# The opening of a one-layer backbone step: order of loads, norm products and the first two FFN chunks

## The chip, the cores and the metric

One core of one Trainium2 chip. The metric is the device time of one execution in microseconds (us). An execution is one launch that computes the whole step. TensorE (PE in the rows) does the matrix products, VectorE (DVE), ScalarE (ACT) and GpSimd (POOL) the rest; SyncE (SP) and ACT issue DMAs. MB is 1,048,576 bytes: each weight tile that is loaded is one.

## The reference, cut to what matters

One layer over 128 context tokens and 128 latent tokens, width 2048, fp32:

```
mod = silu(c) @ ada_w + ada_b            # 9 vectors of 2048 per token group
x += 0.5 * g1 * swiglu(rms_norm(x) * w * (1 + sc1) + sh1)      # FFN 1, hidden width 5632
z  = (rms_norm(x) * w * (1 + sc2) + sh2) @ w_in  -> mLSTM, attention, merge, w_out
x += g2 * mix
x += 0.5 * g3 * swiglu(rms_norm(x) * w * (1 + sc3) + sh3)      # FFN 2
swiglu(h) = (silu(g) * u) @ wo   with g, u = split(h @ wi, 2)
```

The change touches only the start: the modulation vectors sc1 and sh1, the first norm, and the first two column chunks (512 wide) of g and u of FFN 1.

## The kernel before, in words

**Units and tiles.** A weight tile `raw_w` is 512 rows by 512 columns, 1 MB, four slots. Each tile makes two units. Every product is done in three single passes: the weight is split into `w_hi` (ACT, line 1278) and `w_lo` (DVE, line 1731), the activation into `xT_hi` and `xT_lo`, and a unit (line 672) is 2 row blocks by 2 token groups by 3 matmuls: 12 matmuls of 512 columns, over 256 rows of the contraction. `w_hi` and `w_lo` have four slots, so a unit's split waits for the product four units earlier. SP may issue the load of a raw tile when both units of the tile four before it are split (`tile`, line 389).

**The modulation chunks.** A chunk of `ada_w` (2048 by 512) is four tiles of 1 MB, called quarters of the chunk here, ada 0 to ada 8. `ada_q(c, q)` (line 592) is the product of one of them with the conditioning vectors, 4 matmuls with 32 weight columns (8 records in the trace). After the fourth, DVE adds the bias (`ada_rows`), PE selects two rows (`ada_sel`), DVE copies (`ada_blk`), PE transposes (`ada_T`), DVE copies to columns (`ada_cols`). `ada_w_sb` has one slot per quarter, so the load of a quarter waits until PE has used the same quarter of the chunk before (`ada_used`, lines 383 and 386); two more slots, `ada_x`, take the first two quarters of ada 3, 5 and 7.

**The first FFN in four quarters.** Quarter q of the model width (512 of 2048) needs ada 2q and 2q+1: they give the scale and the shift of this quarter's part of x. So `norm0_quarter(q)` (DVE line 1817, ACT line 1330) makes `acol`, modulates `xm`, and splits it into `xT_hi` and `xT_lo`; only then can PE run the units of the quarter. On DVE the order is: acol, xm, the split of the quarter's first unit, `xT_lo`. PE's `prologue` (line 761) runs, for each q, six units (G0, U0 and G1: gate chunk 0, value chunk 0, gate chunk 1, two units each), between them the products of the two ada chunks of the next quarter, and then, in `second` (line 796), the eight units of U1, value chunk 1, over all four quarters. The accumulators are PSUM banks 0 and 1 (G0, later free), 2 and 3 (U0, later U1), 4 and 5 (G1); bank 6 takes the ada products, bank 7 the selections.

**The start.** ACT issues the small loads (identity, `colrows`, `biasrows`) and then the tokens x; SP issues ada 0 at once. PE transposes `colrows` and `biasrows` when all of the small loads have landed, ACT makes the conditioning vectors (silu), PE runs ada 0, then ACT's sums of squares and DVE's `variance` and `diagonal` give `diag`, and PE makes the normed, transposed tokens as products with `diag` (`norm0`, line 661, eight banks), with ada 1 among them (lines 888 to 905).

**What sets the order.** It is all written out by hand: each engine works its own list in order, and waits at semaphores. SP's list of loads is lines 413 to 427: ada 0, ada 1, three tiles, ada 2, ada 3, three tiles, and so on, then ada 8 in halves between the four tiles of U1. A load that must wait holds up all loads behind it on SP.

Of the kernel before, what the change touches and what calls it, by code (L numbers as in the profile page):

```python
# [75 lines left out]
QT = 6  # L76
VCH = 4 * SC3
# [66 lines left out]
def build(nc, I, O):  # L144
    ctx = ExitStack()
    with ctx:
# [54 lines left out]
        vec_acc = place("vec_acc", [P, GROUPS, CH], at=SLOT + 32768)  # L201
        assert top[0] <= SCR
# [96 lines left out]
        ctile_zeroed = sem("ctile_zeroed")  # L299
        bias_zeroed, xm_act, acol_ready = sem("bias_zeroed"), sem("xm_act"), sem("acol_ready")  # L300
# [66 lines left out]
        def _(sp):  # L367
# [30 lines left out]
            def ffn(f, t0):  # L398
# [14 lines left out]
                if f == 0:  # L413

                    for q in range(4):
                        ada_load(2 * q)
                        if q == 0:
                            sp.wait_ge(bias_zeroed, 1)
                            bias(0)
                        ada_load(2 * q + 1)  # L420
                        for n, col in enumerate((0, D_FF, CH)):
                            tile(t0 + 3 * q + n, 0, rows(wi, q)[:, :, col:col + CH])
                    for q in range(4):
                        if q < 2:
                            ada_load(ADA_PRE, (2 * q, 2 * q + 1))
                        tile(t0 + 12 + q, 0, rows(wi, q)[:, :, CH + D_FF:2 * CH + D_FF])
                    ffn_out(0, t0 + 16, 0)
                else:
                    ffn_in(0, t0, 0)
# [161 lines left out]
        def _(pe):  # L591
# [114 lines left out]
            def ffn(f, u0, stage):  # L706
# [55 lines left out]
                def prologue():  # L762

                    for q in range(4):
                        a, b = 2 * q + 2, 2 * q + 3
                        for m in range(QT):
                            if q < 3 and m == 4:
                                if q == 0:
                                    pe.wait_ge(xn_act, 4)
                                ada_sel(a, a)  # L770
                                ada_q(b, 0)
                                ada_T(a)
                                for r in range(1, 4):
                                    ada_q(b, r)
                            kb = 4 * q + 2 * (m % 2)
                            pe.wait_ge(xT_lo_ready, kb // 2 + 1)
                            for half in range(2):
                                if q < 3 and m == 4 and half == 1:
                                    ada_sel(b, b)
                                unit(u0 + QT * q + m, 0, xT_hi, xT_lo, kb, 2 * (m // 2), kb == 0, kb == KD - 2, (half,))  # L780
                                if q == 0 and m == 2 and half == 0:
                                    ada_q(a, 2)
                                if q == 0 and m == 2 and half == 1:
                                    ada_q(a, 3)
                                if 0 < q < 3 and m == 3 and half == 0:
                                    ada_q(a, m)
                            if q < 3 and m == 4:
                                ada_T(b)
                            if q == 0 and m == 0:
                                pe.wait_ge(xn_dve, 4)  # L790
                            if q < 3 and m < (3 if q else 2):
                                ada_q(a, m)
                            if q == 3 and m >= 4:
                                ada_q(ADA_PRE, m - 4)

                def second():

                    def u_between(k):
                        if k < 2:
                            ada_q(ADA_PRE, k + 2)  # L800
                        if k == 1:
                            pe.wait_ge(silu_done, 2)
                            h_transposes(0)

                    pe.wait_ge(h_done, 1)
                    x_chunk(u0 + 24, 0, 2, u_between)
                    ffn_out(0, u0 + 32, 0)
                    ada_sel(ADA_PRE, ADA_PRE)
                    h_transposes(1)

                if f == 0:
                    prologue()
                    second()
# [75 lines left out]
            pe.wait_ge(rows_landed, 96)  # L889
            pe.transpose(ps[:, 0, 0:80], colrows[:, :], cst[0:80, C_ID:C_ID + 80])  # L890
            pe.transpose(ps[:, 0, 80:188], biasrows[:, :], cst[0:108, C_ID:C_ID + 108]).then_inc(cols_ps, 1)
            pe.wait_ge(cond_silu, 1)
            pe.wait_ge(one_ready, 1)
            ada_acc(0)
            ada_sel(0, 0)
            ada_T(0)
            norm0(range(4))
            ada_acc(1)
            ada_sel(1, 1)
            norm0(range(4, 6))  # L900
# [365 lines left out]
        def _(act):  # L1266
# [63 lines left out]
            def norm0_quarter(q):  # L1330
# [4 lines left out]
                split(QT * q, 0)  # L1335
# [12 lines left out]
                split(QT * q + 1, 0)  # L1348
# [41 lines left out]
            def ffn(f, u0):  # L1390
# [47 lines left out]
                def prologue():  # L1438

                    for q in range(4):  # L1440
                        norm0_quarter(q)
                        if q == 0:
                            xn_copy(3)
                        for m in range(2, QT):
                            split(u0 + QT * q + m, 0)
                    act.wait_ge(units_done, u0 + 20)
# [1002 lines left out]
```

## Time and profile before

| | |
|---|---|
| time, median of 3 runs | 2241.32 us (2240.49 to 2242.13) |
| span of the profiled execution, first to last instruction | 2238.6 us |
| median time less that span | 2.7 us |
| PE busy | 2209.0 us, 99% |
| DVE busy | 1606.5 us, 72% |
| ACT busy | 935.3 us, 42% |
| read from memory | 543.71 MB (decimal), 244 GB/s over the span |
| granted TensorE clock, mean | 0.999 |

The profiled execution's own time is not given apart from its span; the 2.7 us around the span are the launch and the end, as far as the median tells. A busy share counts an engine as busy until the modelled end of its instruction; for a matmul of 512 columns that is 0.39 us, while the next one starts 0.23 us after it. So the start times are what to read on PE, and an idle time in the rows is a little shorter than the gap between the starts.

### The profile page before, as it was taken

How to read it: one execution, taken by the hardware profiler on the slowest of the kernel's cores; microseconds unless marked ns; L12 is line 12 of the kernel's file. 1: busy time of each engine (PE TensorE's matmuls, PEld its weight loads, DVE VectorE, ACT ScalarE, POOL GpSimd, SP SyncE). 2: the span in 40 equal slices, each digit the busy share in tenths (PEclk: the TensorE clock that was granted, in tenths of full speed). 3: DMA queues.
4: the chain of work that ended last, by engine and by line, in shares of the span. 5: the costliest groups of instructions: out<-in, count | busy, mean ns of one | idle time of the engine just before them, and what ended most of it. 6: DMA issues, size and time to landing. Idle time of an engine off the chain costs nothing.

```text
span 2238.6 us, 28359 instructions
## 1 busy us (share of the span) xinstructions
PE 2209.0 (99%) x10498; PEld 1773.5 (79%) x10498; DVE 1606.5 (72%) x1858; ACT 935.3 (42%) x1099; POOL 64.5 (3%) x55
## 2 busy tenths in 40 slices
PE   6999999999999999999999999999999999999999
PEld 3567877878778778888888888888888888888887
DVE  3447888878887879756867887885567676776756
ACT  3334333333333336445544444454434443444443
POOL 0010000000000000000600000100000000000000
PEclk9999999999999999999999999999999999999999
DMA  9998888778888786655536776746675757557563
GB/s 371 387 326 312 283 315 299 278 278 302 308 280 291 276 267 211 215 163 167 185 113 227 260 264 228 269 162 207 221 241 193 261 191 258 192 188 262 188 225 131
DMA packets 273332, 548.13 MB, mean 245 GB/s; under 512 B 9014, under 2 KB 9418, under 8 KB 273008
## 3 DMA queue, kind: packets, MB, share of 16 engines
q1 hardware_dynamic: 212388, 421.59, 55.2%
q10 hardware_dynamic: 57772, 115.57, 14.4%
q0 software_dynamic: 3104, 10.05, 1.6%
q8 instruction: 45, 0.74, 0.1%
q14 instruction: 23, 0.19, 0.0%
HBM read 543.71 MB, written 3.46 MB: 244 GB/s over the span
## 4 chain that ended last, share of the span: by engine, by line
PE 96%; DMA 2%; DVE 2%; ACT 1%; issue 0%; SPq 0%; ACTq 0%; DVEq 0%
PE ps L681 30%; PE ps L683 29%; PE ps L682 29%; DMA ada_w_sb<-in_ada_w 2%; PE ps L618 1%; PE ps L603 1%; PE ps L758 1%; PE ps L627 1%; PE ps L668 0%; PE ps L1032 0%; PE ps L1100 0%; DVE w_lo L1731 0%; PE ps L635 0%; PE ps L1108 0%; DVE xm L1846 0%
## 5 line engine op out<-in xcount | busy, mean ns | idle before, releaser
L1278 ACT CAST w_hi<-raw_w 128x1024 fp32r<-128x1024 f32 x728 | 764.7, 1053 | 1169.4 <-PE ps L683 1110.9
L1731 DVE TENSOR_TENSOR w_lo<-raw_w,w_hi 128x1024 fp32r<-128x1024 f32 x728 | 897.3, 1236 | 442.9 <-ACT w_hi L1278 438.9
L681 PE MATMUL ps<-w_hi,xT_hi 128*128 128x512 f32 x2080 | 821.4, 395 | 4.2 <-DVE xT_lo L1814 3.4
L683 PE MATMUL ps<-w_hi,xT_lo 128*128 128x512 f32 x2080 | 810.5, 390 | 0.0
L682 PE MATMUL ps<-w_lo,xT_hi 128*128 128x512 f32 x2080 | 810.0, 389 | 0.0
L681 PEld LDWEIGHTS ps<-w_hi,xT_hi 128*128 128x128 f32 x2080 | 390.8, 188 | 110.3 <-issue 25.0
L683 PEld LDWEIGHTS ps<-w_hi,xT_lo 128*128 128x128 f32 x2080 | 390.5, 188 | 82.9
L682 PEld LDWEIGHTS ps<-w_lo,xT_hi 128*128 128x128 f32 x2080 | 390.9, 188 | 78.4
L1786 DVE SCALAR_TENSOR_TENSOR vec_acc<-ada_w_sb,ctile,vec_acc 128x512 f32<-128x512 f32 x420 | 299.1, 745 | 0.0
L681 PE MATMUL ps<-w_hi,hT_hi 128*128 128x512 f32 x704 | 276.2, 392 | 0.0
L683 PE MATMUL ps<-w_hi,hT_lo 128*128 128x512 f32 x704 | 274.2, 390 | 0.0
L682 PE MATMUL ps<-w_lo,hT_hi 128*128 128x512 f32 x704 | 273.9, 389 | 0.0
L683 PEld LDWEIGHTS ps<-w_hi,hT_lo 128*128 128x128 f32 x704 | 132.1, 188 | 27.8
L681 PEld LDWEIGHTS ps<-w_hi,hT_hi 128*128 128x128 f32 x704 | 132.2, 188 | 26.9 <-issue 0.2
L682 PEld LDWEIGHTS ps<-w_lo,hT_hi 128*128 128x128 f32 x704 | 132.2, 188 | 26.8
L1936 DVE TENSOR_TENSOR acc<-acc,ps 128x1024 f32<-128x1024 f32 x72 | 87.9, 1221 | 48.3 <-PE ps L683 48.3
L681 PE MATMUL ps<-w_hi,hcT_hi 128*128 128x512 f32 x128 | 50.1, 391 | 0.0
L683 PE MATMUL ps<-w_hi,hcT_lo 128*128 128x512 f32 x128 | 49.9, 390 | 0.0
L682 PE MATMUL ps<-w_lo,hcT_hi 128*128 128x512 f32 x128 | 49.8, 389 | 0.0
L1786 DVE SCALAR_TENSOR_TENSOR vec_m<-ada_m,ctile,vec_m 128x512 f32<-128x512 f32 x60 | 43.2, 746 | 0.0
L512 POOL DMA_DIRECT2D gate_dram<-gate_rows x3 | 1.6, 538 | 1414.8 <-DVE gate_rows L1742 1414.8
L603 PE MATMUL ps<-ada_w_sb,ctile 128*32 128x512 f32 x240 | 35.4, 678 | 7.1 <-DMA ada_w_sb<-in_ada_w 6.8
(279 smaller groups left out, 1036.8 us busy)
## 6 DMA issues: line engine op xcount, KB each, us to landing
raw_w<-in_ffn_wi SPq DMA_DIRECT2D x176, 1024.0 KB, 5.1
ada_w_sb<-in_ada_w ACTq DMA_DIRECT2D x96, 1024.0 KB, 8.2
raw_w<-in_ffn_wo SPq DMA_DIRECT2D x88, 1024.0 KB, 5.2
raw_w<-in_w_in SPq DMA_DIRECT2D x68, 1024.0 KB, 5.3
ada_w_sb<-in_ada_w SPq DMA_DIRECT2D x30, 1024.0 KB, 12.5
raw_w<-in_w_out SPq DMA_DIRECT2D x16, 1024.0 KB, 5.3
ada_m<-in_ada_w ACTq DMA_DIRECT2D x12, 1024.0 KB, 5.3
raw_w<-in_w_proj_m SPq DMA_DIRECT2D x8, 1024.0 KB, 5.3
```

What stands on the lines that cost most here:

```text
L512: pool.dma_start(gate_dram[r].rearrange("k g p -> (k g) p"), gate_rows[:, at, :]).then_inc(gate_stored, 16)
L603: mm = pe.matmul(ps[32 * j:32 * j + 32, 6, :], ctile[:, 4 * q + j, :], w[:, q, j, :], start=(q == 0), stop=(q == 3))
L618: mm = pe.matmul(ps[32 * j:32 * j + 32, 6, :], ctile[:, 4 * q + j, :], ada_w_sb[:, t, j, :], start=(q == 0), stop=(q == 3))
L627: mm = pe.transpose(ps[:, bank + g, b * P:(b + 1) * P], vec[:, g, b * P:(b + 1) * P], ident)
L681: pe.matmul(out, a_hi, w_hi[:, slot, kk, :], start=(first and kk == 0), stop=False)
L682: pe.matmul(out, a_hi, w_lo[:, slot, kk, :], start=False, stop=False)
L683: mm = pe.matmul(out, a_lo, w_hi[:, slot, kk, :], start=False, stop=(last and kk == 1))
L758: mm = pe.transpose(ps[:, 4 + b // 2, (b % 2) * TOK + g * P:(b % 2) * TOK + (g + 1) * P], h[:, g, b * P:(b + 1) * P], ident)
L1278: act.copy(w_hi[:, us % SPL, :, :], raw_w[:, slot, 2 * half:2 * half + 2, :]).then_inc(hi_ready, 1)
L1731: dve.tensor_tensor(w_lo[:, us % SPL, :, :], raw_w[:, slot, 2 * half:2 * half + 2, :], w_hi[:, us % SPL, :, :].bitcast(F32), ALU.subtract) ...
L1786: ins = dve.scalar_tensor_tensor(acc[:, g, :], w, scale, acc[:, g, :], ALU.mult, ALU.add)
L1936: dve.tensor_tensor(acc[:, :, c], acc[:, :, c], ps[:, banks:banks + 2, :], ALU.add).then_inc(acc_done, 1)
```

## The change

In words:

- The tokens are issued by SP ahead of ada 0 (they were issued by ACT behind the small loads). The bias rows have a semaphore and a PSUM bank of their own, so that the conditioning vectors wait only for `colrows`.
- The norm products of banks 0 to 3 run between the second and third quarter of ada 0, bank 4 and 5 around the selection of ada 0, then ada 1, then bank 6 and 7. DVE makes `diag` ahead of `ada_rows(0)`.
- The tiles of the first two FFN chunks come in a new order (`PRE_TILES`). Quarter 0 runs G0, U0 and U1; then U1, G0, U0 of quarter 1; then G1 of quarters 0 and 1; then G0, U0, G1 of quarter 2 and of quarter 3; then U1 of quarters 2 and 3. The quarters' first units are 0, 6, 16 and 22 (they were 0, 6, 12 and 18).
- U1 of quarters 0 and 1 is summed in banks 4 and 5, ACT copies it to `u1_half`, and G1 takes the banks. U1 of quarters 2 and 3 is summed in banks 2 and 3, and DVE adds the two halves in an instruction of its own ahead of `h`.
- SP's list becomes: x, ada 0, ada 1, tiles 0 to 2, ada 2, ada 3, tiles 3 to 6, ada 4, tile 7, ada 5, tiles 8 to 10, ada 6, ada 7, tiles 11 to 15, ada 8.
- On PE ada 4 and ada 5 stand among units 10 to 14, ada 6 and 7 among 16 to 21. The transposes of ada 3 and ada 7 stand behind units 5 and 21.

```diff
+PRE_TILES = ((0, G_0), (0, U_0), (0, U_1), (1, U_1), (1, G_0), (1, U_0), (0, G_1), (1, G_1),
+             (2, G_0), (2, U_0), (2, G_1), (3, G_0), (3, U_0), (3, G_1), (2, U_1), (3, U_1))
+Q_UNIT = (0, 6, 16, 22)
+PRE_BANKS = {G_0: 0, U_0: 2, G_1: 4, U_1: 4}
...
+                    sp.dma_start(x[:, CTX, :], I["x_prompt"][0]).then_inc(x_landed, 16)
+                    sp.dma_start(x[:, LAT, :], I["x_sample"][0]).then_inc(x_landed, 16)
+                    ada_load(0)
+                    sp.wait_ge(bias_zeroed, 1)
+                    bias(0)
+                    ada_load(1)
+                    pre_tiles(0, 3)
+                    ada_load(2)
+                    ada_load(3)
+                    pre_tiles(3, 7)
+                    ada_load(4)
+                    pre_tiles(7, 8)
+                    ada_load(5)
+                    pre_tiles(8, 11)
+                    ada_load(6)
+                    ada_load(7)
+                    pre_tiles(11, 16)
+                    ada_load(ADA_PRE)
...
+                    whole(0)
+                    pe.wait_ge(xn_dve, 4)
+                    whole(1)
+                    ada_q(2, 0)
+                    whole(2)
+                    ada_q(2, 1)
+                    whole(3)
+                    ada_q(2, 2)
+                    ada_q(2, 3)
+                    pe.wait_ge(xn_act, 4)
+                    pre_unit(4, 0)
+                    ada_sel(2, 2)
+                    ada_q(3, 0)
+                    ada_T(2)
+                    pre_unit(4, 1)
+                    ada_q(3, 1)
+                    ada_q(3, 2)
+                    ada_q(3, 3)
+                    whole(5)
+                    ada_sel(3, 3)
+                    ada_T(3)
+                    whole(6, 7, 8, 9)
+                    ada_q(4, 0)
+                    whole(10)
+                    ada_q(4, 1)
+                    whole(11)
+                    pe.wait_ge(u1_half_copied, 1)
+                    whole(12)
+                    ada_q(4, 2)
+                    ada_q(4, 3)
+                    pre_unit(13, 0)
+                    ada_sel(4, 4)
+                    pre_unit(13, 1)
+                    ada_q(5, 0)
+                    ada_T(4)
+                    for r in range(1, 4):
+                        ada_q(5, r)
+                    under_two(5, 14)
+                    for m in range(16, 20):
+                        whole(m)
+                        ada_q(6, m - 16)
+                    pre_unit(20, 0)
+                    ada_sel(6, 6)
+                    ada_q(7, 0)
+                    ada_T(6)
+                    for r in range(1, 4):
+                        ada_q(7, r)
+                    pre_unit(20, 1)
+                    ada_sel(7, 7)
+                    whole(21)
+                    ada_T(7)
+                    whole(22, 23, 24, 25, 26, 27)
+                    pe.wait_ge(h_done, 1)
+                    whole(28, 29)
+                    pe.wait_ge(silu_done, 2)
+                    h_transposes(0)
+                    ada_q(ADA_PRE, 0)
+                    ada_q(ADA_PRE, 1)
+                    whole(30)
+                    ada_q(ADA_PRE, 2)
+                    ada_q(ADA_PRE, 3)
+                    whole(31)
                     ffn_out(0, u0 + 32, 0)
...
+            ada_q(0, 0)
+            ada_q(0, 1)
+            norm0(range(4))
+            ada_q(0, 2)
+            ada_q(0, 3)
+            norm0(range(4, 5))
+            pe.wait_ge(biascol_copied, 3)
             ada_sel(0, 0)
+            norm0(range(5, 6))
             ada_T(0)
             ada_acc(1)
             ada_sel(1, 1)
             ada_T(1)
             norm0(range(6, 7))
...
+                        if q == 1:
+                            act.wait_ge(units_done, u0 + 8)
+                            act.copy(u1_half[:], ps[:, 4:6, :]).then_inc(u1_half_copied, 1)
...
+                    dve.tensor_tensor(u1_half[:], u1_half[:], ps[:, 2:4, :], ALU.add).then_inc(u1_summed, 1)
...
+                    dve.tensor_tensor(h[:], sg[:], u1_half[:], ALU.mult).then_inc(h_done, 1)
```

`whole(m)` is one unit, `pre_unit(m, half)` half of one, and `under_two(c, m)` is half of unit m, `ada_sel(c)`, the other half, `ada_T(c)` and unit m + 1.

## Rows read from the trace of the kernel before

**Rows 1.** The page: busy time, and the 40 equal slices of 56 us.
```profile
PE 2209.0 (99%) x10498; PEld 1773.5 (79%) x10498; DVE 1606.5 (72%) x1858; ACT 935.3 (42%) x1099; POOL 64.5 (3%) x55
...
PE   6999999999999999999999999999999999999999
...
DMA  9998888778888786655536776746675757557563
```

**Rows 2.** Stages by time: length, engines' busy time, granted clock, DMA share, GB/s.
```profile
0.00:25.00 25.00, 9.19 (x43) 1.67 (x43) 4.34 (x20) 8.39 (x22) 0.20 (x4) 1.00 0.96 355
...
75.00:100.00 25.00, 22.88 (x130) 11.81 (x128) 6.97 (x15) 2.89 (x4) 0.00 (x0) 0.93 1.05 387
...
125.00:150.00 25.00, 24.05 (x111) 17.34 (x110) 14.65 (x19) 14.95 (x18) 0.89 (x1) 1.00 1.05 387
150.00:175.00 25.00, 25.00 (x121) 18.97 (x120) 11.97 (x11) 9.08 (x9) 6.56 (x11) 1.00 0.87 256
```

**Rows 3.** PE's timeline, opening: start us, us, instruction, idle before it and releaser.
```profile
19.72 1.94 PE L603 MATMUL ps<-ada_w_sb,ctile 128*32 128x512 f32 x8 [0.78 <-DMA ada_w_sb<-in_ada_w]
...
25.73 5.79 PE L668 MATMUL ps<-diag,x 128*128 128x128 f32 x32 [1.66 <-DVE diag L1805]
31.45 3.64 PE L603 MATMUL ps<-ada_w_sb,ctile 128*32 128x512 f32 x32
...
41.79 0.50 PE L681 MATMUL ps<-w_hi,xT_hi 128*128 128x512 f32 x1 [1.59 <-DVE xT_lo L1814]
...
61.59 1.06 PE L603 MATMUL ps<-ada_w_sb,ctile 128*32 128x512 f32 x8 [0.36 <-DMA ada_w_sb<-in_ada_w]
...
69.64 0.50 PE L681 MATMUL ps<-w_hi,xT_hi 128*128 128x512 f32 x1 [0.59 <-DVE xT_lo L1814]
...
88.67 1.06 PE L603 MATMUL ps<-ada_w_sb,ctile 128*32 128x512 f32 x8 [0.47 <-DMA ada_w_sb<-in_ada_w]
91.39 1.93 PE L603 MATMUL ps<-ada_w_sb,ctile 128*32 128x512 f32 x8 [1.66 <-DMA ada_w_sb<-in_ada_w]
...
100.96 0.50 PE L681 MATMUL ps<-w_hi,xT_hi 128*128 128x512 f32 x1 [0.58 <-DVE xT_lo L1814]
...
121.21 1.06 PE L603 MATMUL ps<-ada_w_sb,ctile 128*32 128x512 f32 x8 [0.84 <-DMA ada_w_sb<-in_ada_w]
...
129.29 0.50 PE L681 MATMUL ps<-w_hi,xT_hi 128*128 128x512 f32 x1 [0.58 <-DVE xT_lo L1814]
...
132.70 0.47 PE L681 MATMUL ps<-w_hi,xT_hi 128*128 128x512 f32 x1 [0.36 <-DVE w_lo L1731]
...
173.88 0.39 PE L681 MATMUL ps<-w_hi,hT_hi 128*128 128x512 f32 x1
```

**Rows 4.** PE's timeline: two ada products around one unit, a transpose of ada.
```profile
72.58 1.07 PE L603 MATMUL ps<-ada_w_sb,ctile 128*32 128x512 f32 x8
...
76.53 1.06 PE L603 MATMUL ps<-ada_w_sb,ctile 128*32 128x512 f32 x8
...
97.34 0.27 PE L642 MATMUL ps<-cst,ada_rows_sb 128*128 128x128 f32 x1
```

**Rows 5.** SP's timeline: start us, us over all, DMA issues.
```profile
12.70 9.39 SPq L387 DMA_DIRECT2D ada_w_sb<-in_ada_w  x4
...
81.61 2.95 SPq L387 DMA_DIRECT2D ada_w_sb<-in_ada_w  x2
```

**Rows 6.** The page's DMA issues: count, KB each, median us to landing.
```profile
raw_w<-in_ffn_wi SPq DMA_DIRECT2D x176, 1024.0 KB, 5.1
```

**Rows 7.** ACT's timeline: the first and the last of eight sums of squares.
```profile
16.22 0.63 ACT L1319 ACTIVATE sg<-x 128x512 f32<-128x512 f32 x1 [4.06 <-DMA x<-in_x_sample]
...
20.52 0.61 ACT L1319 ACTIVATE sg<-x 128x512 f32<-128x512 f32 x1
```

**Rows 8.** DVE's timeline: the second product of silu and value.
```profile
174.20 1.21 DVE L2032 TENSOR_TENSOR h<-sg,ps 128x1024 f32<-128x1024 f32 x1
```

**Rows 9.** A short stretch with its granted clock, columns as in rows 2.
```profile
92.00:94.00 2.00, 2.00 (x10) 0.66 (x3) 0.61 (x1) 0.00 (x0) 0.00 (x0) 0.50 1.05 388
```

More of the change, by code:

```diff
@@ L201, in build @@
         vec_acc = place("vec_acc", [P, GROUPS, CH], at=SLOT + 32768)
+        u1_half = place("u1_half", [P, GROUPS, CH], at=SLOT + 32768)
         assert top[0] <= SCR
@@ L413, in ffn, with pre_tiles @@
                 if f == 0:
[L415 to L426, printed above, removed]
+                    def pre_tiles(first, end):
+                        for n in range(first, end):
+                            q, col = PRE_TILES[n]
+                            tile(t0 + n, 0, rows(wi, q)[:, :, col:col + CH])
+                    sp.dma_start(x[:, CTX, :], I["x_prompt"][0]).then_inc(x_landed, 16)
[16 more added lines that the diff above has]
+                    ada_load(ADA_PRE)
                     ffn_out(0, t0 + 16, 0)
@@ L762, in prologue @@
                 def prologue():
[L764 to L803, printed above, removed]
-                    pe.wait_ge(h_done, 1)
-                    x_chunk(u0 + 24, 0, 2, u_between)
+                    def pre_unit(m, half):
+                        q, col = PRE_TILES[m // 2]
+                        kb = 4 * q + 2 * (m % 2)
+                        pe.wait_ge(xT_lo_ready, kb // 2 + 1)
+                        first, last = kb == 0 or (col, kb) == (U_1, KD // 2), kb == KD - 2 or (col, kb) == (U_1, KD // 2 - 2)
+                        banks = 2 if col == U_1 and q > 1 else PRE_BANKS[col]
+                        return unit(u0 + m, 0, xT_hi, xT_lo, kb, banks, first, last, (half,))
@@ new lines, in whole, with under_two @@
+                    def whole(*ms):
+                        for m in ms:
+                            pre_unit(m, 0)
+                            mm = pre_unit(m, 1)
+                        return mm
+                    def under_two(c, m):
+                        pre_unit(m, 0)
+                        ada_sel(c, c)
+                        pre_unit(m, 1)
+                        ada_T(c)
+                        whole(m + 1)
+                    whole(0)
+                    pe.wait_ge(xn_dve, 4)
@@ L812, in ffn @@
                     prologue()
-                    second()
                 else:
@@ L1443, in prologue @@
                             xn_copy(3)
-                        for m in range(2, QT):
-                            split(u0 + QT * q + m, 0)
-                    act.wait_ge(units_done, u0 + 20)
+                        for m in range(Q_UNIT[q] + 2, Q_UNIT[q] + QT):
+                            split(u0 + m, 0)
+                        if q == 1:
+                            act.wait_ge(units_done, u0 + 8)
+                            act.copy(u1_half[:], ps[:, 4:6, :]).then_inc(u1_half_copied, 1)
+                            for m in range(12, 16):
+                                split(u0 + m, 0)
+                    act.wait_ge(units_done, u0 + 24)
                     act.activation(sg[:], ps[:, 0:2, :], ACT.Silu).then_inc(silu_done, 1)
-                    for u in range(24, 24 + AHEAD):
-                        split(u0 + u, 0)
-                    act.wait_ge(units_done, u0 + 24)
+                    for m in range(28, 28 + AHEAD):
+                        split(u0 + m, 0)
+                    act.wait_ge(units_done, u0 + 28)
                     act.wait_ge(h_done, 1)
                     act.activation(sg[:], ps[:, 4:6, :], ACT.Silu).then_inc(silu_done, 1)
-                    for k in range(16):
-                        split(u0 + 24 + AHEAD + k, 0)
-                        if k == 2:
+                    for m in range(28 + AHEAD, 40 + AHEAD):
+                        split(u0 + m, 0)
+                        if m == 33:
                             hT_hi_of(0)
-                        if k == 4:
+                        if m == 35:
                             act.wait_ge(ada_used, 4 * VCH1)
@@ L2008, in prologue @@
                         norm0_quarter(q)
-                        for m in range(2, QT):
-                            split(u0 + QT * q + m, 0)
+                        for m in range(Q_UNIT[q] + 2, Q_UNIT[q] + QT if q != 1 else Q_UNIT[2]):
+                            split(u0 + m, 0)
                         if q < 3:
@@ L2083, in _ @@
                 xn_copy(n)
+            ada_rows(0, 0, 16)
+            xn_copy(2)
+            ada_blk(0)
+            ada_cols(0)
             ada_rows(1, 1, 16)
             ada_blk(1)
-            xn_copy(2)
             ada_cols(1)
```

57 lines of the change are left out of this document (28 added, 29 removed).

## The prediction

> **What bounds the kernel now.** I read the page first: PE is busy 99% of the span, and of its 40 slices only the first is under 9 tenths [rows 1]. So all that an edit of the opening can give is PE's lost time in the first 150 us. The stages by time come next: up to 150 us the DMA share is 1.05 at 387 GB/s, its full rate, and PE has holes; from 150 us PE is busy 25.00 of 25 us [rows 2]. So there are two bounds, one behind the other: first the stream of loads, then PE without a gap to the end. A microsecond that PE gets ahead by the end of the opening is one off the total, and a microsecond lost there stays lost.
>
> PE's timeline shows the holes [rows 3]. Until the first unit at 41.79 it waits for loads, for diag and for xT_lo. From the first unit of quarter 1 (69.64) to the first unit of the output product (173.88) it takes 104.24 us, in which the holes are 0.47, 1.66 and 0.84 (a quarter of ada not landed), 0.58 twice (xT_lo of quarters 2 and 3) and 0.36 (w_lo): 4.49. To this comes time at half clock: the ada product at 91.39 takes 1.93, not 1.06, and the stage 92 to 94 has a granted clock of 0.50, 1.2 of 2.4 GHz [rows 3, 9]. With some 0.65 on the first matmuls of the next unit that is 1.5. So 6.0 us are lost, and 98.2 are work.
>
> **The stream of loads sets the quarters.** The last quarter of ada 3 is the 21st MB, that of ada 5 the 32nd, that of ada 7 the 43rd (2 of x, 4 per chunk of ada, 3 tiles per quarter). PE was released by them at 61.59, 91.39 and 121.21 [rows 3]: 29.8 us per 11 MB, 2.71 per MB. Quarter 1 starts 8.05 after the first of these.
>
> **The change part by part.**
>
> *Start.* The tokens go ahead of ada 0, so the sums of squares, 16.22 to 21.1 before [rows 7], can start at about 10 to 12, and diag is there at some 16.6 to 18.7 (25.7 before). PE's norm products then fill holes between the quarters of ada 0. ada 1 still ends as the 10th MB, at 19.72 + 4 x 2.71 = 30.6 at the earliest. The four ada 1 products, 31.45 to 35.1 before, now end at about 31.6, the transpose follows at once, and the first unit comes some 4 us earlier, at 37 to 38. Yet this buys nothing: quarter 1 hangs on ada 3, and ada 3 is still the 21st MB. PE already waited for it by 0.36; it will wait about 2. I take nothing for the whole start, though it moves 9 us of idle time.
>
> *A cost in it.* SP may load quarter 3 of ada 1 only when PE has used quarter 3 of ada 0. In the kernel before SP issued its four loads from 12.70 on and the share never fell [rows 5, 2]. Now 32 norm products (5.79 us, half of them slow [rows 3]) stand ahead of that use, which comes at diag (16.6 to 18.7) + 5.8 + 1.0 = 23.4 to 25.5. A load into an empty stream takes 5.1 us to land [rows 6]: 28.5 to 30.6, against 27.9 in an unbroken stream. So the stream stops for 0.6 to 2.7 us, and everything behind it on SP with it. It could be 0 if x lands very early. I take 1.5.
>
> *Quarter 0.* Now unit 5 runs ahead of the selection and transpose of ada 3, so nothing covers the chain behind the transpose. From the landing of ada 3: product 1.0, unit 5 with its start 2.84, selection to copy 0.6, copy to transpose to columns 0.7, and from columns to the first unit 3.3. That is 8.4 against 8.05: +0.4, and a hole of about 3.3 in place of 0.59. Bounds 0 to 0.9.
>
> *Quarter 1.* Ten units and ada 4 and 5. From unit 6 at about 70 (plus the 1.5): a unit with an ada product takes 3.95 (76.53 less 72.58 [rows 4]), without 2.73. So ada_q(4,2) comes after 7 units and 2 products, at some 93.3 (it was 81.5). SP must wait for it with quarter 3 of ada 5, whose issue was at 81.61 [rows 5]; with the quarters 1 and 2 of ada 5 landed by 91.2, the stream runs dry for some 3 us, and ada 5 ends at 101.2, not 96.6. PE arrives there at 100.5: a wait of 0.7. From then all loads are late, and the last of ada 7, now the 45th MB, comes at 101.2 + 11 x 2.71 = 131.0, where PE is at 129.9: 1.1. Together 1.8 us; 0 if the stream doesn't stop, up to 3.4 if issue costs more. This takes the place of 0.47 + 1.66 + 0.84 and the 1.5 at half clock.
>
> *Quarter 2 to 3.* Between transpose of ada 5 and unit 16 stands one unit, as before: 0.58. But ada 7's transpose stands behind unit 21 with nothing after it. From a transpose to the next quarter's first unit 3.62 pass (97.34 to 100.96 [rows 3, 4]), so PE stands for 3.35 where it stood 0.58. That is the largest new hole.
>
> *Small terms.* Units 6 to 9 and 22 to 27 follow without an ada product between the first two, so the w_lo wait of 0.36 [rows 3] comes twice. ada 8 and part of ada 4 run in pairs (1.0 each rather than 1.2): -0.7, bounds 0 and -1.2.
>
> *u1_half.* ACT's copy of two banks (about 1.05) is done long before unit 12 asks for it. DVE's addition (1.2, as h [rows 8]) comes behind unit 31, then h; PE's second part of the output product asks for h two units, 5.5 us, later, and 2.6 are needed. Nothing; were the cover gone, 1.2. Nor does ada 8 at the end of SP's list matter: with all stops it has landed by 160, and PE uses it from 162 on.
>
> *Sum against the span of 2238.6.* Start 0; stop of the stream +1.5; quarter 0 +0.4; from quarter 1 on the holes are 0.58 + 3.35 + 0.72 + 1.8 - 0.7 = 5.75 in place of 6.0: -0.25. Together +1.65. The profiled span lies 2.7 under the median of the timed runs, and I carry the difference over: 2241.3 + 1.65 = 2243.0. The low end of the terms (no stop, no late ada) is 0.4 + 4.65 - 0.7 - 6.0 = -1.65; the high end, 0.4 + 2.7 + 0.58 + 3.35 + 0.72 + 3.4 - 0.7 - 6.0, is +4.45.
>
> **The rivals.**
>
> *The reordering works as a whole.* Behind the last quarter's release now 11.5 units are left, not 15.5: 10.9 us less work behind a landing that is 2 MB, 5.4 us, later. Read so, the gain would be 5.5. It speaks for this that the DMA waits are the longest holes. Against it: only 6.0 us are lost at all from quarter 1 on, and 3.35 of new waiting is written into the order. With the stream unbroken I get -1.65, 2239.7; with the new hole shrunk to 0.58 as well -4.4, 2236.9. Chance 0.17.
>
> *SP stands behind PE (slower).* The place is SP's wait for ada_q(0,2) and ada_q(4,2), the price is each stop in full (up to 2.7 and 3.4), and it decides once the stops add up to over 3 us: +4.45, 2245.8. For it: SP's list is strictly in order. Against: the share held at 1.05 through all of its waits so far. Chance 0.16.
>
> *Half clock.* In the opening PE fell to 1.2 GHz once, at about 91.5, after waits of 0.47 and 1.66 with one ada product between them, and was back at full clock by 96 [rows 3, 9]; the xT_lo wait of 1.59 at 41.79 brought no fall. The new holes of 3.3 are longer than any after 41.79. If one brings a fall like that one, +1.5; if both do, +3: 2244.5 or 2246.0. Chance 0.17.
>
> The Trainium skill ("TensorE: Matmul & The Clock Gate", What's actually happening) says that half rate is the default state and that activity alone lifts it, so idle stretches send the clock back. The trace agrees in the one case that it has. By that rule the longer holes should each cost this; by the row of 41.79 a hole alone doesn't.
>
> **How the numbers follow.** The forecast (stops of 1 to 3 us, both holes, no fall) has 0.50, its own range 2241 to 2244.5. About 0.2%, 4.5 us, is what a measurement can tell from no change. Faster than 2236.8 needs the first rival and more: 0.07. Slower than 2245.8 takes the second rival's upper half, both falls, or a mix: 0.17. The rest, 0.76, is within. The range is 2238.0 to 2247.5: it takes in the low sum and most of a stop with a fall.
>
> **What would show it.** First unit at 37 to 39 (41.79 before) but the first unit of quarter 1 at 69.5 to 72. A dip of the DMA share near 25 us and near 91 to 96. PE idle about 3.3 ahead of unit 6 and of unit 22, released by xT_lo, the latter at 140 to 142. First output unit at 174 to 177 (173.88 before). No change of PE after it. I am wrong if quarter 1 starts clearly before 69, if the share stays at 1.05 to 130, or if something after 175 us moves.

## The result, and the profile after

| | before | changed |
|---|---|---|
| median of 8 runs | 2241.01 us | 2247.09 us |
| lowest to highest | 2240.29 to 2242.13 | 2245.12 to 2248.30 |
| span of the profiled execution | 2238.6 us | 2243.2 us |

The changed kernel is slower: ratio 1.0026, 95% interval 1.0017 to 1.0035, +6.1 us. The forecast was 2243.0. The profiled execution of the changed kernel is the quickest of its eight (2245.12); its span is 4.6 above that of before, and the trace accounts for these 4.6. The other runs of it have spans up to 2246.4. Time less span is 1.7 to 2.1 us in the runs on record, not the 2.7 that the text ahead of the prediction gives; there a span and a median of different executions were compared.

PE's timeline of the changed kernel, the lines that answer to [rows 3] (start us, us, instruction, idle before it and releaser; the changed kernel has line 623 for 603, 688 for 668, 701 for 681):

```profile
18.22 5.29 PE L688 MATMUL ps<-diag,x 128*128 128x128 f32 x32 [1.62 <-DVE diag L1877]
...
33.73 1.07 PE L623 MATMUL ps<-ada_w_sb,ctile 128*32 128x512 f32 x8 [2.88 <-DMA ada_w_sb<-in_ada_w]
...
63.57 1.07 PE L623 MATMUL ps<-ada_w_sb,ctile 128*32 128x512 f32 x8 [0.60 <-DMA ada_w_sb<-in_ada_w]
...
72.04 0.50 PE L701 MATMUL ps<-w_hi,xT_hi 128*128 128x512 f32 x1 [3.35 <-DVE xT_lo L1886]
...
105.57 1.07 PE L623 MATMUL ps<-ada_w_sb,ctile 128*32 128x512 f32 x8 [1.64 <-DMA ada_w_sb<-in_ada_w]
113.65 0.50 PE L701 MATMUL ps<-w_hi,xT_hi 128*128 128x512 f32 x1 [0.58 <-DVE xT_lo L1886]
135.22 1.06 PE L623 MATMUL ps<-ada_w_sb,ctile 128*32 128x512 f32 x8 [0.81 <-DMA ada_w_sb<-in_ada_w]
...
144.64 0.79 PE L701 MATMUL ps<-w_hi,xT_hi 128*128 128x512 f32 x1 [3.35 <-DVE xT_lo L1886]
...
178.44 0.39 PE L701 MATMUL ps<-w_hi,hT_hi 128*128 128x512 f32 x1
```

The last line is the one to start from: the output product begins at 178.44, not 173.88, 4.56 later, and the whole span is 4.6 longer. So nothing behind it moved, and everything is in the opening. Quarter 1 starts at 72.04 (69.64 before): +2.4. From there to the output product it is 106.40 (104.24 before): +2.16.

Short stages of the changed kernel (columns as in [rows 2]: length, busy of PE, PEld, DVE, ACT, POOL, granted clock, DMA share, GB/s):

```profile
24.00:26.00 2.00, 2.00 (x22) 0.86 (x15) 0.57 (x1) 0.13 (x1) 0.00 (x0) 1.00 0.55 126
26.00:28.00 2.00, 2.00 (x26) 1.51 (x28) 1.01 (x3) 0.07 (x1) 0.00 (x0) 1.00 0.89 312
...
36.00:38.00 2.00, 1.58 (x14) 1.32 (x7) 1.03 (x5) 1.05 (x1) 0.00 (x0) 0.50 1.06 389
...
56.00:58.00 2.00, 2.00 (x14) 1.05 (x6) 0.69 (x1) 0.00 (x0) 0.00 (x0) 1.00 0.52 122
...
72.00:74.00 2.00, 1.96 (x6) 1.51 (x6) 0.69 (x1) 1.97 (x5) 0.00 (x0) 0.62 1.06 387
74.00:76.00 2.00, 2.00 (x6) 1.61 (x5) 1.91 (x2) 1.95 (x3) 0.00 (x0) 0.52 1.04 385
...
94.00:96.00 2.00, 2.00 (x15) 1.13 (x17) 1.05 (x1) 0.00 (x0) 0.00 (x0) 1.00 0.00 0
```

Two things are new. The first is the stream of loads. In the kernel before its share was 0.92 or more in every stage of 2 us from 20 to 154 us. Now the loads stop three times while PE still depends on them: at 24 to 28, at 56 to 58, and at 92 to 98 (the share is 0.00 in the stage shown). A fourth stop at 144 to 150 comes when no later row of the opening has a wait for a load. The second is the clock. Right behind the hole of 3.35 ahead of unit 6 most of the time is at 1.2 GHz (granted 0.62 and 0.52 in the two stages shown); the same follows behind the hole ahead of unit 22 (granted 0.54 in 144 to 146). There is a third such stretch ahead of both, from 34 to 41 us (0.50 in 36 to 38), behind the wait of 2.88 for ada 1. SP's timeline says what it stood behind in the second and the third stop:

```profile
55.87 1.23 SPq L396 DMA_DIRECT2D ada_w_sb<-in_ada_w  x2
...
77.89 4.60 SPq L393 DMA_DIRECT2D ada_x<-in_ada_w  x2
96.48 1.23 SPq L396 DMA_DIRECT2D ada_w_sb<-in_ada_w  x2
```

The pair at 55.87 is quarters 3 and 4 of ada 3, which wait for the products of ada 2 behind unit 3. From 82.5 to 96.5 SP issues nothing. The pair at 96.48 is quarters 3 and 4 of ada 5; in the kernel before they went out from 81.61 on [rows 5]. They wait for the products of ada 4 behind unit 12.

### The profile page after: what moved, and what is told of

Read it like the earlier page. It is cut to its first block, busy times and chain, and to the rows that moved or that the text cites. A ratio compares the mean times of both kernels' runs of the same rounds, so it can differ in the third digit from the quotient of the medians.

```text
span 2243.2 us, 28403 instructions
## 1 busy us (share of the span) xinstructions
PE 2209.6 (99%) x10498; PEld 1777.6 (79%) x10498; DVE 1608.3 (72%) x1859; ACT 936.4 (42%) x1100; POOL 64.5 (3%) x55
## 4 chain that ended last, share of the span: by engine, by line
PE 96%; DMA 2%; DVE 1%; ACT 1%; issue 0%; ACTq 0%; DVEq 0%
PE ps L701 30%; PE ps L703 29%; PE ps L702 29%; PE ps L638 1%; DMA ada_w_sb<-in_ada_w 1%; PE ps L623 1%; PE ps L778 1%; PE ps L647 1%; PE ps L688 0%; ACT sg L1388 0%; PE ps L1101 0%; PE ps L1169 0%; DMA colrows<-in_norm_ffn_w 0%; PE ps L655 0%; PE ps L1177 0%; DVE xm L1918 0%
```

## The experiments

The figures are medians of 11 runs (9 of e12), against the median of the kernel before on the same chip; the intervals of the ratios are about 0.0009 to each side, 2 us. So a difference between two experiments of under 2 us rests on their runs and traces more than on its interval.

| kernel | median us | against before | ratio, 95% interval |
|---|---|---|---|
| changed kernel | 2247.09 | +6.1 | 1.0026 (1.0017 to 1.0035) |
| e1 norm products behind ada 0 | 2245.24 | +4.2 | 1.0017 (1.0008 to 1.0026) |
| e2 both transposes early | 2244.01 | +2.9 | 1.0012 (1.0003 to 1.0021) |
| e3 ada 4 used early | 2245.42 | +4.4 | 1.0019 (1.0010 to 1.0028) |
| e4 holes filled | 2244.56 | +3.5 | 1.0017 (1.0008 to 1.0026) |
| e5 start alone | 2243.61 | +2.4 | 1.0010 (1.0001 to 1.0019) |
| e6 last transpose early | 2244.66 | +3.5 | 1.0015 (1.0006 to 1.0024) |
| e7 four edits | 2239.17 | -2.0 | 0.9992 (0.9983 to 1.0001) |
| e8 four edits and fill | 2237.51 | -3.7 | 0.9984 (0.9975 to 0.9993) |
| e9 as e8, old start | 2240.51 | -0.8 | 0.9998 (0.9989 to 1.0007) |
| e10 as e8, ada 3 in unit 5 | 2236.51 | -4.8 | 0.9980 (0.9971 to 0.9989) |
| e11 mended start alone | 2240.88 | -0.4 | 0.9999 (0.9990 to 1.0009) |
| e12 as e10, ada 7 in unit 20 | 2235.51 | -5.8 | 0.9975 (0.9965 to 0.9985) |

**e1: the first stop.**

```diff
-            ada_q(0, 0)
-            ada_q(0, 1)
-            norm0(range(4))
-            ada_q(0, 2)
-            ada_q(0, 3)
-            norm0(range(4, 5))
+            ada_acc(0)
+            norm0(range(5))
```

> The changed kernel with one edit: all four products of ada 0 ahead of the norm products (banks 0 to 4 then run behind them). Theory (stream stop): SP waits for quarter 3 of ada 0 to be used, so the stop of the load stream at 24 to 28 us goes, ada 3 lands at about 61.6 instead of 63.6, the first unit of quarter 1 starts at about 70.0 instead of 72.0, and the time falls by 2 us, to about 2245. Rival (the start is covered by the later stops and costs nothing): the landing of ada 3 moves, but unit 22 stays at 144.6 and the time within 0.5 us of 2247.

Measured: 2245.24, 1.9 less than the changed kernel. The share stays at 1.04 to 1.07 from 22 to 42 us. PE's timeline of e1:

```profile
38.96 0.50 PE L701 MATMUL ps<-w_hi,xT_hi 128*128 128x512 f32 x1 [1.56 <-DVE xT_lo L1882]
...
62.18 1.06 PE L623 MATMUL ps<-ada_w_sb,ctile 128*32 128x512 f32 x8 [0.76 <-DMA ada_w_sb<-in_ada_w]
...
70.66 0.79 PE L701 MATMUL ps<-w_hi,xT_hi 128*128 128x512 f32 x1 [3.35 <-DVE xT_lo L1882]
```

ada 3 lands at 62.18 instead of 63.57, 1.4 of the 2.0 us. The second stop is still there: the share is 0.60 in 54 to 56. But the edit shrank that one too, because the first unit starts at 38.96 instead of 40.50, and SP issues the last two quarters of ada 3 at 54.31 instead of 55.87. So the 1.4 are not the first stop's alone. In this trace unit 22 starts at 144.56, as late as in the changed kernel, which is what the rival said; the medians went with the theory. The clock tells where the lead went in this execution: behind unit 6 the granted clock is 0.50 in all three stages from 70 to 76 and 0.80 in the next, about twice the stretch of the changed kernel, and the first product of ada 4 comes at 84.64, where it came at 84.74. One profiled execution of each is too little to settle how much of the 1.9 survives the later stops.

**e2 and e6: the transposes.** In e2 both chunks are selected and transposed under half a unit and one unit; in e6 only the last one.

```diff
-                    pre_unit(20, 0)
                     ada_sel(6, 6)
                     ada_q(7, 0)
                     ada_T(6)
                     for r in range(1, 4):
                         ada_q(7, r)
-                    pre_unit(20, 1)
-                    ada_sel(7, 7)
-                    whole(21)
-                    ada_T(7)
+                    under_two(7, 20)
```

> The changed kernel with the selections of ada 3 and ada 7 inside units 4 and 20, behind all their products, and the transposes ahead of units 5 and 21, so that one unit covers the chain to xT_lo. Theory (two holes, and half clock behind each): holes of 3.35 ahead of unit 6 and unit 22 become 0.6; counted from the landing of the chunk the quarter starts 8.05 later instead of 8.5 and 9.4, so 0.4 + 1.4 us, and with the holes go both stretches at half clock, 1.8 us each: together -5.4, to about 2241.7. Rival (the clock falls anyway, from the waits for ada and the ada products themselves): -1.8 only, to about 2245.3, with a granted clock under 1 still seen after 72 and after 143.

> The changed kernel with only the second of the two edits of the run with both transposes early: the selection of ada 7 inside unit 20, the transpose ahead of unit 21; quarter 0 as in the changed kernel. Theory (the hole ahead of unit 22 costs 1.4 us as counted from the landing, and half clock 0.8 net behind it): -2.2, to about 2244.9, and the run with both edits gained the rest of its 3.1 elsewhere. Rival (the other edit, in quarter 0, which put quarter 1 at 74.3 instead of 72.0 us in that run, was a loss of up to 2): more than -3.1, under 2244.

Measured: 2244.01 and 2244.66, 3.1 and 2.4 less than the changed kernel. e6 met its expectation of 2.2. e2 missed its 5.4: with unit 4 behind the products of ada 3, PE reaches them a unit (2.7 us) sooner and only waits for the loads; ada 3's last product is at 63.78, it runs at half clock (1.94), and quarter 1 starts at 74.31, 2.3 later than in the changed kernel. In both, unit 22 has 0.58 us idle ahead of it and no fall of the clock behind it. PE's timeline of e2, then of e6:

```profile
63.78 1.94 PE L623 MATMUL ps<-ada_w_sb,ctile 128*32 128x512 f32 x8 [1.64 <-DMA ada_w_sb<-in_ada_w]
...
74.31 0.50 PE L701 MATMUL ps<-w_hi,xT_hi 128*128 128x512 f32 x1 [0.60 <-DVE xT_lo L1878]
```

```profile
143.96 0.50 PE L701 MATMUL ps<-w_hi,xT_hi 128*128 128x512 f32 x1 [0.58 <-DVE xT_lo L1882]
```

**e3: the third stop.**

```diff
                     ada_q(4, 0)
-                    whole(10)
                     ada_q(4, 1)
-                    whole(11)
-                    pe.wait_ge(u1_half_copied, 1)
-                    whole(12)
+                    whole(10)
                     ada_q(4, 2)
                     ada_q(4, 3)
+                    whole(11)
+                    pe.wait_ge(u1_half_copied, 1)
+                    whole(12)
```

> The changed kernel with the products of ada 4 in pairs behind units 9 and 10 instead of behind 9, 10 and 12. Theory (SP stands behind the use of ada 4): the stop of the stream at 92 to 98 us shrinks by 5 us of issue time to nothing or 1 us, PE's waits of 1.64 at 105.6 and 0.81 at 135.2 go, up to 2.4 us less work time lost, though PE may wait a little for ada 4 itself: -1 to -2.4, to about 2245. Rival (PE has slack there): the dip goes but the time stays within 0.5 us.

Measured: 2245.42, 1.7 less. The stage 94 to 96 of e3, which was at 0.00 in the changed kernel:

```profile
94.00:96.00 2.00, 2.00 (x10) 1.66 (x9) 0.24 (x1) 1.05 (x1) 0.00 (x0) 1.00 1.05 398
```

```profile
132.59 1.06 PE L623 MATMUL ps<-ada_w_sb,ctile 128*32 128x512 f32 x8 [0.21 <-DMA ada_w_sb<-in_ada_w]
142.00 0.79 PE L701 MATMUL ps<-w_hi,xT_hi 128*128 128x512 f32 x1 [3.35 <-DVE xT_lo L1886]
```

PE no longer waits for ada 5, the wait for ada 7 is 0.21 instead of 0.81, and unit 22 starts at 142.00 instead of 144.64. The theory holds. Half of this lead is gone by the output product, which starts at 177.18 instead of 178.44: behind this hole half clock lasted from 141 to 148 in e3, about twice as long as in the changed kernel.

**e4: hole or clock.** Six products that nobody reads go into each of the two holes.

```diff
+                    def fill():
+                        for r in range(6):
+                            pe.matmul(ps[:, 6, 0:2 * P], ident, x[:, CTX, 0:2 * P], start=True, stop=True)
...
                     ada_T(3)
+                    fill()
...
                     ada_T(7)
+                    fill()
```

> The changed kernel with six extra products (identity by 256 columns of x into a free part of bank 6, never read) behind the transposes of ada 3 and of ada 7, about 2.8 us in each of the two holes of 3.35. They do nothing for the result and leave the order, the loads and the chain to xT_lo as they are. Clock theory: PE stays at full clock behind both holes, and the time falls by 1.8 us for each, 3.6 in all, to about 2243.5, while unit 6 and unit 22 start as before relative to the transposes. Rival (the holes themselves are the whole cost): no change, or slower by what the extra products add, 0 to 0.5 us.

Measured: 2244.56, 2.5 less. This is the experiment that separates waiting from clock, since the order, the loads and the chain are the same. The two executions differ at the start, though (e4 has no stretch at half clock from 34 to 41, and its ada 3 lands 0.7 later), so they are compared from unit 6 on. A stage of e4 and four starts of its PE timeline:

```profile
74.00:76.00 2.00, 1.85 (x9) 1.16 (x7) 1.81 (x3) 2.00 (x3) 0.00 (x0) 1.00 1.05 386
```

```profile
72.79 0.50 PE L701 MATMUL ps<-w_hi,xT_hi 128*128 128x512 f32 x1 [0.76 <-DVE xT_lo L1892]
...
113.36 0.50 PE L701 MATMUL ps<-w_hi,xT_hi 128*128 128x512 f32 x1 [0.60 <-DVE xT_lo L1892]
...
144.45 0.50 PE L701 MATMUL ps<-w_hi,xT_hi 128*128 128x512 f32 x1 [0.75 <-DVE xT_lo L1892]
...
177.53 0.39 PE L701 MATMUL ps<-w_hi,hT_hi 128*128 128x512 f32 x1
```

The granted clock is 1.00 in both places. From unit 6 to unit 16 it takes 40.57 instead of 41.61, from unit 22 to the output product 33.08 instead of 33.80: 1.76 for the two falls in these executions, against 3.6 expected. Part of the gap is this: at half clock PE is late for the second unit, so the w_lo wait that comes there at full clock (0.37 and 0.36 in e4, none in the changed kernel) is swallowed. The rest of the gap stays open.

**e5 and e11: the start in the old order.** Both are the kernel before with the start of the changed kernel alone (tokens first, bias rows apart, diag early). e5 has the norm products between the quarters of ada 0, e11 has `ada_acc(0)` and `norm0(range(5))` there, as e1.

> The kernel before with the start of the changed kernel alone (tokens first on SP, bias rows apart, norm products between the quarters of ada 0 and around its selection, diag ahead of ada_rows), and the old order of tiles, units and ada products from the first unit on. Theory (the start buys nothing and stops the stream once): a dip of the DMA share at 24 to 28 us, the first unit at about 40, ada 3 landed 1.5 to 2 us later, quarter 1 at about 71.5 instead of 69.6, and the time up by 1.5 to 2, to about 2243. Rival (the earlier first unit pays): the time stays at 2241 or falls by up to 1.2, the lead of the first unit.

> The kernel before with the start alone, as in the run of the start alone, but with all products of ada 0 ahead of the norm products. In the kernel before the products of ada 2 stand behind the first half of unit 2 at the latest, so SP never waits for them and ada 3 is bound by the stream. Theory (the earlier first unit is only of use where the ada 2 products stand behind unit 3, as in the new order): no dip of the share at 24 to 28 us, first unit at about 38.5, quarter 1 at 69.6 as before, time within 0.5 us of 2241.2. Rival (the start gives the 3 us here too): 2238 to 2239.

Measured: 2243.61, +2.4, and 2240.88, -0.4. PE's timeline of e5, then of e11:

```profile
64.43 1.06 PE L606 MATMUL ps<-ada_w_sb,ctile 128*32 128x512 f32 x8 [1.64 <-DMA ada_w_sb<-in_ada_w]
72.51 0.50 PE L684 MATMUL ps<-w_hi,xT_hi 128*128 128x512 f32 x1 [0.58 <-DVE xT_lo L1821]
```

```profile
39.01 0.50 PE L684 MATMUL ps<-w_hi,xT_hi 128*128 128x512 f32 x1 [1.56 <-DVE xT_lo L1817]
...
61.92 1.07 PE L606 MATMUL ps<-ada_w_sb,ctile 128*32 128x512 f32 x8 [1.63 <-DMA ada_w_sb<-in_ada_w]
70.00 0.50 PE L684 MATMUL ps<-w_hi,xT_hi 128*128 128x512 f32 x1 [0.58 <-DVE xT_lo L1817]
```

With the stop quarter 1 starts 2.9 late, where 1.5 to 2 were expected. Without it the first unit is at 39.01, 2.8 us ahead of before, and quarter 1 is at 70.00 where it was at 69.64: the lead is spent in waits for ada 3. In this order the start is worth nothing, as forecast. One premise of e11's expectation is not right: SP does wait for the products of ada 2 in the old order. The fourth stands behind all of unit 2 (at 53.89 in the kernel before), and SP issues the last two quarters of ada 3 from 52.42 on, when the third product (51.29) is through. But the share stays at 0.99 or above there, so this wait costs nothing.

**e7 and e8: the losses mended.** e7 has the edits of e1, e3 and e6, and this one; e8 has `fill()` behind it.

```diff
-                    whole(5)
+                    pre_unit(5, 0)
                     ada_sel(3, 3)
+                    pre_unit(5, 1)
                     ada_T(3)
```

> The changed kernel with four edits: all products of ada 0 ahead of the norm products; ada 4 in pairs behind units 9 and 10; the selection of ada 7 inside unit 20 and its transpose ahead of unit 21; the selection of ada 3 inside unit 5 with the transpose still behind it. Theory (the losses add): -1.9, -1.7 and -2.2 as measured or counted for each, -0.4 for the last: -6.2, to about 2240.9, no better than the kernel before. If what the new order of tiles was to bring (four units fewer behind the last landing) shows once the stops and the hole are gone, the first output unit comes at 171 instead of 173.9 and the time is about 2238. Rival (the losses overlap, since each stop hides behind the next): 2243 or more.

> The same four edits, and six extra products (never read) behind the transpose of ada 3, in the one hole that is left, of about 3.3 us ahead of unit 6. Clock theory: no half clock behind this hole, 0.9 us net less than without them. Rival: no change.

Measured: 2239.17 and 2237.51: 7.9 less than the changed kernel where 6.2 were expected, and 1.7 for the fill where 0.9 were. e7's interval still touches 1, e8's doesn't. The changed kernel's order of tiles now beats the kernel before by 3.7 us. PE's timeline of e8, and the three stages of e7 behind its hole:

```profile
61.72 1.06 PE L623 MATMUL ps<-ada_w_sb,ctile 128*32 128x512 f32 x8 [1.17 <-DMA ada_w_sb<-in_ada_w]
...
69.79 0.50 PE L701 MATMUL ps<-w_hi,xT_hi 128*128 128x512 f32 x1 [0.75 <-DVE xT_lo L1884]
...
129.47 1.06 PE L623 MATMUL ps<-ada_w_sb,ctile 128*32 128x512 f32 x8 [1.12 <-DMA ada_w_sb<-in_ada_w]
...
170.59 0.39 PE L701 MATMUL ps<-w_hi,hT_hi 128*128 128x512 f32 x1
```

```profile
70.00:72.00 2.00, 2.00 (x5) 1.61 (x6) 0.72 (x2) 1.97 (x4) 0.00 (x0) 0.50 1.05 384
72.00:74.00 2.00, 2.00 (x7) 1.52 (x6) 2.00 (x2) 1.83 (x2) 0.00 (x0) 0.50 1.05 390
74.00:76.00 2.00, 2.00 (x6) 1.59 (x5) 1.47 (x2) 0.49 (x1) 0.00 (x0) 0.50 1.05 387
```

The output product starts at 170.59, 3.3 ahead of the kernel before. e7's fall is longer than that of the changed kernel (0.50 through three stages, where that one had 0.62 and 0.52), and from quarter 1 to unit 16 e7 takes 40.73 (69.93 to 110.66), e8 38.49 (69.79 to 108.28): 2.2 us for one fall, 1.7 in the medians. The eleven runs of e8 lie within 0.7 us (2237.16 to 2237.89), the eight of the changed kernel within 3.2.

**e9: the old start under the new order.** It is e8 with the start of the kernel before.

> The kernel with the four edits and the extra products, but with the start of the kernel before (tokens on ACT behind the small loads, bias rows with them, norm products behind ada 0). Theory (quarter 1 hangs on ada 3, the 21st MB, and the start buys nothing): the first unit comes at about 41.8 instead of 38.1, quarter 1 still at 69.8, time within 0.5 us of 2237.5. Rival (a part of the gain is the start's): slower by 1 to 3.7 us, the lead of the first unit.

Measured: 2240.51, 3.0 more than e8. My theory fell, and with it a step of the prediction. PE's timeline and two stages of e9:

```profile
65.15 1.06 PE L621 MATMUL ps<-ada_w_sb,ctile 128*32 128x512 f32 x8 [0.77 <-DMA ada_w_sb<-in_ada_w]
73.22 0.50 PE L699 MATMUL ps<-w_hi,xT_hi 128*128 128x512 f32 x1 [0.75 <-DVE xT_lo L1882]
```

```profile
54.00:56.00 2.00, 2.00 (x10) 1.50 (x8) 0.00 (x0) 0.00 (x0) 0.00 (x0) 1.00 0.13 43
56.00:58.00 2.00, 2.00 (x17) 0.42 (x16) 0.00 (x0) 0.00 (x0) 0.00 (x0) 1.00 0.00 0
```

SP's timeline of e9:

```profile
57.27 1.23 SPq L396 DMA_DIRECT2D ada_w_sb<-in_ada_w  x2
```

In the new order the last two products of ada 2 stand behind unit 3. SP may load the last two quarters of ada 3 only then. With the first unit at 41.97 that is at 57.3, the stream has run dry, and ada 3 lands 3.4 late. With the first unit at 38.06 the share falls only to 0.86 in 54 to 56. So the new order needs the earlier first unit, though the old one has no use for it (e11).

**e10 and e12: transposes between the halves of a unit.** e10 has `ada_T(3)` ahead of `pre_unit(5, 1)` and four extra products; e12 the same with ada 7 in unit 20.

> The kernel with the four edits and the extra products (four instead of six), with selection and transpose of ada 3 both between the halves of unit 5. Quarter 1 should start 1.0 earlier, at 68.7 instead of 69.8. Theory (behind it the stream of loads is the bound: PE waited 1.12 for ada 7 at 129.5): the landing of ada 7 and unit 22 stay where they are, PE waits 2 us there, time within 0.4 us of 2237.5. Rival (PE is the bound from quarter 1 on): -1.0, to 2236.5.

> The kernel with the four edits, four extra products and ada 3 in unit 5, and now the transpose of ada 7 between the halves of unit 20 too. From the landing of ada 7 to unit 22 it takes 8.05 with 0.58 of it idle ahead of unit 22; the early transpose costs a wait of 0.4 for DVE's copy and covers the chain by 1.4 more. Theory: -0.2 us net, to 2236.3, at most -0.6. Rival (unit 22 waits for something else, a tile or w_lo): no change or slower.

Measured: 2236.51 and 2235.51, 1.0 less each time. PE's timeline of e10, then of e12:

```profile
128.46 1.06 PE L623 MATMUL ps<-ada_w_sb,ctile 128*32 128x512 f32 x8 [0.99 <-DMA ada_w_sb<-in_ada_w]
...
169.58 0.39 PE L701 MATMUL ps<-w_hi,hT_hi 128*128 128x512 f32 x1
```

```profile
129.35 1.06 PE L623 MATMUL ps<-ada_w_sb,ctile 128*32 128x512 f32 x8 [1.01 <-DMA ada_w_sb<-in_ada_w]
...
169.60 0.39 PE L701 MATMUL ps<-w_hi,hT_hi 128*128 128x512 f32 x1
```

In e10 I expected nothing, because PE waited for ada 7. But ada 7 landed at 128.46 instead of 129.47: SP issues those loads when PE has used the chunk before, so the stream came earlier with PE. In e12 it takes 40.25 from the last product of ada 7 (129.35) to the output product (169.60), where e10 takes 41.12 (128.46 to 169.58); I had expected 0.2. e12 is the quickest kernel of the case, 5.8 us under the kernel before.

## Why the prediction came out as it did

It said no clear change with a lean to slower. The time fell in its range, but 0.4 under the upper end, outside the forecast's own range, and above 2245.8, a part to which it gave 0.17. The case that happened is the sum of two rivals. In the spans 4.6 us were lost and 1.65 forecast: 0.5 of the difference lies ahead of quarter 1 and 2.4 behind it.

- *What bounds the kernel.* Right: the start of the output product and the span moved by the same 4.6.
- *The signs.* Right: the dips of the share near 25 and behind 91, the idle 3.3 ahead of units 6 and 22, and no change behind the opening. Missed: the first unit came at 40.50 (37 to 39 forecast), quarter 1 at 72.04, just past 72, unit 22 at 144.64 (140 to 142), the output product at 178.44 (174 to 177). The time for the first unit left out the forecast's own stop: PE waited 2.88 for the last of ada 1, which came at 33.73 and not at 30.6. Without the stop the first unit is at 38.06 to 38.96 (e8, e1).
- *The stop of the stream.* Right in place and cause, and sized 1.5 for a landing that came 2.0 later. But there are two stops ahead of ada 3. The one at 24 to 28 was named; the one at 56 to 58, where SP waits for the ada 2 products behind unit 3, was not, though the working on ada 4 used the same rule. e1 and e9 show it. Which of the two sets the landing differs between executions: e3, e4 and e6, with the same start as the changed kernel, have a share of 0.95 to 0.99 in 56 to 58, and ada 3 lands at 63.67 to 64.29. The 5.1 us that the working took for a load into an empty stream are the median of all `raw_w` loads; no run isolates such a load.
- *"I take nothing for the whole start".* Right for the old order (e11: -0.4) and wrong as a general step: in the new order the earlier first unit shrinks the second stop, worth 3.0 us (e9 against e8). The step looked at which load releases quarter 1, and not at which use of PE releases the load.
- *Quarter 0.* From landing to unit 6 it takes 8.47, forecast 8.4, and the hole is 3.35, forecast 3.3.
- *Quarter 1.* Waits of 1.64 and 0.81, 2.45 against 1.8 forecast. Place and cause are right (e3). That the size came so near is in part luck: ada 5 had landed at 105.57 and not at 101.2, but PE too was late, and began to wait at 103.93 and not at 100.5.
- *Quarter 2 to 3.* The hole is 3.35, as forecast.
- *The clock.* This is the term that was left out. I gave 0.50 to no fall and 0.17 to this rival; both holes brought one. In the changed kernel, e1, e3, e6 and e7 every hole of 3.35 did, 8 of 8. The same holes filled, in e4, e8 and e9, 4 in all, brought none. The early fall at 34 to 41, behind the wait for ada 1, was in no rival; what it cost isn't separated. I took the wait of 1.59 that brought no fall as evidence against; it is half as long as the holes. The Trainium skill ("TensorE: Matmul & The Clock Gate", What's actually happening) says that half rate is the default and comes back with idleness; these 8 holes bear it out.
- *The small terms.* The two w_lo waits of 0.36 are there at full clock (e4) and not in the changed kernel; the 1.76 of e4 is already net of them.
- *The sum.* From quarter 1 on +2.16 against -0.25: 0.65 are the longer waits, 1.76 the two falls as e4 measures them. Together 2.4, the whole difference. e4, without the falls, takes 104.74 from quarter 1 to the output product, +0.50: 0.57 above the forecast are its waits for loads (1.53 and 0.84 against 1.8), 0.2 all the other terms.
- *u1_half.* Hidden, as forecast. DVE's timeline of the changed kernel:

```profile
178.64 1.22 DVE L2103 TENSOR_TENSOR u_half<-u_half,ps 128x1024 f32<-128x1024 f32 x1 [1.88 <-PE ps L703]
179.99 1.23 DVE L2107 TENSOR_TENSOR h<-sg,u_half 128x1024 f32<-128x1024 f32 x1
```

h is done at 181.2, and PE, which asks for it 5.5 us behind 178.44, shows no idle time there.

- *The first rival*, that the reordering works as a whole, was no mistake in the idea: e7 and e8 show that it does once the stops are short and the hole ahead of unit 22 is covered, even with the hole ahead of unit 6 (3.35 in e7, filled in e8) and some dips (0.86 in 54 to 56 and 0.35 in 120 to 122 in e8) left. The prediction was right that this kernel had neither.

**Left open.** The median moved by 6.1, the profiled spans by 4.6. Longer falls in the slower executions would fit in part: from 30 us on, a fall took about 3.4 or about 6.8 us in every trace of the case, and behind unit 6 the long one cost 1.3 more than the short one (2.24 in e7 against e8, 0.92 in the changed kernel against e4 up to the first ada 4 product). But the mean granted clocks on record don't order the eight runs (0.997 in the quickest and in the slowest, 0.996 to 0.998 in the others), and the slower runs have no trace. A later landing of ada 3 would fit as well: 63.57 in the changed kernel's trace is the earliest of the four with this start and unit order. The two stops and the falls weren't separated in every run either: e1, e2 and e3 each bring some of the others along.

## What to carry to other kernels

When a product is moved in an engine's list, look up which load waits for its buffer: here products of ada 0, 2 and 4 that came later on PE each stopped a strictly ordered queue of loads, and the landing that suffered was several MB behind. When an order is changed at the end of a stage, count what covers the chain to the next stage's first operand: a hole of 3.35 us put the next quarter 0.4 us (unit 6: 8.47 behind the landing, not 8.05) or 1.4 us (unit 22: 9.42) later, and half clock behind it cost another 0.7 to 2.2 us. A part of a change that is worth nothing alone can be what another part rests on, so test it in the new order too.

## What the runs showed of the hardware

Unread products in an idle stretch kept TensorE at 2.4 GHz: six of them, 2.75 us, in a hole of 3.35 (e4 twice, e8, e9). Four of them, 1.89 us, stood in the shorter holes of e10 and e12, with no fall either; no run shows these holes unfilled. A fall behind a hole of 3.35 lasted about 3.4 us (changed kernel, 72 to 76) or about 6.8 (e7: granted 0.83 in 68 to 70, 0.50 in 70 to 76, 0.96 in 76 to 78). A shorter wait is erratic: the wait of 1.63 for ada 5 in e11, ahead of which 0.40 and one ada product had passed, brought no fall, and the same pattern 30 us later (0.82, a product, 1.65) did, its product taking 1.93 instead of 1.06. At the start the same waits of 1.62, 0.81 and 0.41 brought a fall in e2, e3 and e6 and none in e4.
